# Splitting the position-bias rows of attention 1 into two fp32r parts

## What is computed

```python
def t5_bucket(dist):
    max_exact = N_BUCKETS // 2
    d = jnp.maximum(dist, 0)
    df = jnp.maximum(d, 1).astype(jnp.float32)
    large = max_exact + (jnp.log(df / max_exact) / math.log(MAX_DISTANCE / max_exact)
                         * (N_BUCKETS - max_exact)).astype(jnp.int32)
    return jnp.where(d < max_exact, d, jnp.minimum(large, N_BUCKETS - 1))

    # moba
    s_own = jnp.einsum('bhqd,bhkd->bhqk', qc, ko).astype(jnp.float32) * scale
    s_own = s_own + jnp.take(tab, t5_bucket(t[:, None] - pos_own[None, :]), axis=1)[None]
    s_own = jnp.where(pos_own[None, :] <= t[:, None], s_own, -jnp.inf)
    # dsa: keys picked by the indexer
    bias = jnp.moveaxis(jnp.take(tab, t5_bucket(t[None, :, None] - idx), axis=1), 0, 1)
    s = jnp.where((idx <= t[None, :, None])[:, None], s + bias, -jnp.inf)
```

## Time and profile before

| | us |
|---|---|
| median of 3 runs | 1678.28 |
| lowest, highest | 1676.63, 1682.06 |
| profiled execution (its span) | 1676.6 |
| PE busy in it | 1630.6 (97%) |
| DVE, ACT, POOL busy | 1226.9, 906.6, 430.5 |
| mean granted PE clock | 0.991 of full speed |

### The profile page before, as it was taken

The page is one execution under the profiler, slowest core; times in us unless marked ns, Lnnn a source line. Parts: engine busy times, 40 slices in busy tenths (PEclk is TensorE's granted clock), DMA queues, the critical chain, the costliest instruction groups (busy, mean ns, idle before and its releaser), DMA issues.

```text
span 1676.6 us, 31268 instructions
## 1 busy us (share of the span) xinstructions
PE 1630.6 (97%) x10740; PEld 1437.4 (86%) x10740; DVE 1226.9 (73%) x2406; ACT 906.6 (54%) x1743; POOL 430.5 (26%) x173
## 2 busy tenths in 40 slices
PE   6999899999999999999999999999999999899998
PEld 3976799999999999888888888965799998579997
DVE  4477879689808994877887777767697887776665
ACT  3455554455459996554545545358544445664443
POOL 0970028989985556000000000000200000020000
PEclk9999999999999999999999999999999999999999
DMA  9885885556553334788888885640388766146553
GB/s 346 295 186 193 304 253 178 186 177 186 178 186 114 114 113 146 255 292 284 292 293 286 287 282 166 184 177 1 130 299 288 275 237 152 55 160 188 186 187 103
DMA packets 105526, 344.24 MB, mean 205 GB/s; under 512 B 18484, under 2 KB 22340, under 8 KB 105445
## 3 DMA queue, kind: packets, MB, share of 16 engines
q1 hardware_dynamic: 101092, 339.19, 61.0%
q10 hardware_dynamic: 4352, 4.02, 0.8%
HBM read 341.02 MB, written 1.10 MB: 204 GB/s over the span
## 4 chain that ended last, share of the span: by engine, by line
PE 90%; DVE 3%; ACT 2%; DMA 2%; POOL 1%; issue 1%; ACTq 0%; POOLq 0%; SPq 0%; DVEq 0%
PE banks L673 26%; PE banks L674 25%; PE banks L675 25%; PE banks L1020 3%; PE banks L868 2%; PE banks L835 1%; DMA ring<-in_stream 1%; POOL weights_low L631 1%; PE banks L886 1%; DVE arena L1870 1%; PE banks L845 1%; ACT weights_high L1308 1%; PE banks L706 1%; PE banks L707 1%; ACT arena L1366 1%
## 5 line engine op out<-in xcount | busy, mean ns | idle before, releaser
L1308 ACT ACTIVATE weights_high<-ring 128x1024 fp32r<-128x1024 f32 x470 | 494.8, 1054 | 312.5 <-PE banks L675 299.0
L631 POOL TENSOR_TENSOR weights_low<-ring,weights_high 128x1024 fp32r<-128x1024 f32 x168 | 429.3, 2569 | 669.2 <-ACT weights_high L1308 668.9
L673 PE MATMUL banks<-ht_high,weights_high 128*128 128x256 f32 x1936 | 556.8, 288 | 4.0 <-DVE ht_low L1825 3.9
L674 PE MATMUL banks<-ht_low,weights_high 128*128 128x256 f32 x1936 | 547.9, 283 | 0.0
L675 PE MATMUL banks<-ht_high,weights_low 128*128 128x256 f32 x1936 | 547.8, 283 | 0.0
L1797 DVE TENSOR_TENSOR weights_low<-ring,weights_high 128x1024 fp32r<-128x1024 f32 x302 | 368.2, 1223 | 86.5 <-ACT weights_high L1308 85.6
L673 PEld LDWEIGHTS banks<-ht_high,weights_high 128*128 128x128 f32 x1936 | 371.2, 192 | 7.6 <-issue 4.8
L674 PEld LDWEIGHTS banks<-ht_low,weights_high 128*128 128x128 f32 x1936 | 371.5, 192 | 2.6
L675 PEld LDWEIGHTS banks<-ht_high,weights_low 128*128 128x128 f32 x1936 | 371.1, 192 | 0.0
L1747 DVE SCALAR_TENSOR_TENSOR arena<-arena,cs 128x1024 f32<-128x1024 f32 x80 | 106.9, 1343 | 36.5 <-DMA arena<-in_ada 31.4
L673 PE MATMUL banks<-weights_high,hidden_high 128*128 128x512 f32 x256 | 100.3, 392 | 0.0
(11 more groups left out here) (275 smaller groups left out, 2580.3 us busy)
## 6 DMA issues: line engine op xcount, KB each, us to landing
ring<-in_stream SPq DMA_DIRECT2D x490, 512.0 KB, 3.5
arena<-in_ada SPq DMA_DIRECT2D x88, 512.0 KB, 5.4
ada_ring<-in_ada SPq DMA_DIRECT2D x56, 512.0 KB, 4.2
arena<-gate_store SPq DMA_DIRECT2D x5, 512.0 KB, 6.0
arena<-bias_rows ACTq DMA_DIRECT2D x1, 2048.0 KB, 19.3
X<-in_x SPq DMA_DIRECT2D x1, 1024.0 KB, 5.9
out<-X SPq DMA_DIRECT2D x4, 256.0 KB, 2.1
arena<-arena ACTq DMA_DIRECT2D x8, 127.5 KB, 4.9
```

The source lines that it names most:

```text
L631: pool.tensor_tensor(WL[:, c % SLOTS, :], ring[:, c % SLOTS, :], WH[:, c % HIGHS, :], ALU.subtract)\
L673: pe.matmul(out, wh, xh, start=start, stop=False, **kw)
L674: pe.matmul(out, wh, xl, start=False, stop=False, **kw)
L1308: act.activation(WH[:, c % HIGHS, :], ring[:, c % SLOTS, :], ACT.Copy).then_inc(S["high_ready"], 1)
```

## The change

The rows are split on DVE right after they are made: a high part rounded to fp32r (`ROWS_HIGH`) and the remainder (`ROWS_LOW`). Both go to DRAM, 2 x 24 KB, and come back shifted, the high part as `BIASH` (2 MB) in the place of `BIAS`, the low part in two loads of 1 MB (`BIASL`: heads of moba, heads of dsa). The flipped identity is copied into fp32r (`FLIP`) ahead of the bf16 masks. Each full fp32 bias product becomes two fp32r products, FLIP by BIASH and FLIP by BIASL.

```diff
-        onehot = sb("onehot", [P, ONEHOTS, 2, 4, P])
+        onehot = at("onehot", "onehot", [P, ONEHOTS, 2, 4, P])
-        bias_rows = nc.dram_tensor("bias_rows", (16, ROW_COLS), F32, kind="Internal")
+        bias_rows = nc.dram_tensor("bias_rows", (2, 16, ROW_COLS), F32, kind="Internal")
-        BIAS = A(A_BIAS, 16, T)
+        BIASH = at("bias_high", "arena", [P, 16, T], F32R, 4 * A_BIAS)
+        BIASL = [at("bias_low_moba", "arena", [P, 8, T], F32R, 4 * A_S), at("bias_low_dsa", "onehot", [P, 8, T], F32R)]
+        FLIP = at("flip", "pick", [P, P], F32R)
+        ROWS_HIGH = at("rows_high", "pick", [P, ROW_COLS], F32R, 4 * 128)
+        ROWS_LOW = at("rows_low", "pick", [P, ROW_COLS], F32R, 4 * 512)
...
# PE, scores
-                        m = pe.matmul(o, flip, BIAS[:, first:first + 3:2, T - w:T], start=False, stop=kind == "moba",
-                                      skip_group_check=True)
+                        low = BIASL[first // 8][:, first % 8:first % 8 + 3:2, T - w:T]
+                        pe.matmul(o, FLIP[:], BIASH[:, first:first + 3:2, T - w:T], start=False, stop=False, skip_group_check=True)
+                        m = pe.matmul(o, FLIP[:], low, start=False, stop=kind == "moba", skip_group_check=True)
...
# PE, ahead of attention 1
-            pe.wait_ge(S["bias_loaded"], 16)
-            pe.wait_ge(S["bf16_ready"], 5)
+            pe.wait_ge(S["bias_loaded"], 48)
+            pe.wait_ge(S["bf16_ready"], 6)
...
# ACT
-            act.dma_start(bias_rows.ap(), A(A_R, ROW_COLS)[0:16, :]).then_inc(S["rows_stored"], 16)
+            for i, rows in enumerate([ROWS_HIGH, ROWS_LOW]):
+                act.dma_start(bias_rows.ap()[i], rows[0:16, :].bitcast(F32)).then_inc(S["rows_stored"], 16)
...
-                act.dma_start(BIAS, shifted).then_inc(S["bias_loaded"], 16)
+                act.dma_start(BIASH[:].bitcast(F32), shifted(0, 16)).then_inc(S["bias_loaded"], 16)
+                for i in range(2):
+                    act.dma_start(BIASL[i][:].bitcast(F32), shifted(16 + 8 * i, 8)).then_inc(S["bias_loaded"], 16)
...
# DVE
-                                      A(A_E, 2 * ROW_COLS)[0:16, ROW_COLS:2 * ROW_COLS], ALU.add).then_inc(S["rows_taken"], 1)
+                                           A(A_E, 2 * ROW_COLS)[0:16, ROW_COLS:2 * ROW_COLS], ALU.add))
+                    link(dve.tensor_copy(ROWS_HIGH[0:16, :], A(A_R, ROW_COLS)[0:16, :]))
+                    dve.tensor_tensor(ROWS_LOW[0:16, :], A(A_R, ROW_COLS)[0:16, :], ROWS_HIGH[0:16, :], ALU.subtract).then_inc(S["rows_taken"], 1)
...
+            dve.tensor_copy(FLIP[:], flip).then_inc(S["bf16_ready"], 1)
             dve.tensor_copy(ident_b[:], ident).then_inc(S["bf16_ready"], 1)
```

More of the change, by code:

```diff
@@ L260, in two_blocks @@
         place, size = {}, 0
-        for name, n in [("arena", NKEYS * T), ("ring", SLOTS * D), ("high", HIGHS * D), ("ht", DB * T), ("hth", DB * T), ("pick", 4 * T)]:
+        for name, n in [("arena", NKEYS * T), ("ring", SLOTS * D), ("high", HIGHS * D), ("ht", DB * T), ("hth", DB * T), ("pick", 4 * T), ("onehot", ONEHOTS * 8 * P)]:
             place[name] = size
@@ L1461, in index_keys, with shifted @@
                 act.activation(small[:, 42:44], small[:, 40:42], ACT.Sqrt, scale=1.0 / 64, bias=epsc[:]).then_inc(S["ik_rms"], 1)
-                act.wait_ge(S["rows_stored"], 16)
-                shifted = bass.AP(tensor=bias_rows, offset=0, ap=[[1, P], [ROW_COLS, 16], [1, T]])
-                act.dma_start(BIAS, shifted).then_inc(S["bias_loaded"], 16)
+                act.wait_ge(S["rows_stored"], 32)
+                def shifted(row, n):
+                    return bass.AP(tensor=bias_rows, offset=row * ROW_COLS, ap=[[1, P], [ROW_COLS, n], [1, T]])
+                act.dma_start(BIASH[:].bitcast(F32), shifted(0, 16)).then_inc(S["bias_loaded"], 16)
+                for i in range(2):
+                    act.dma_start(BIASL[i][:].bitcast(F32), shifted(16 + 8 * i, 8)).then_inc(S["bias_loaded"], 16)
             take("qk1", 18, lambda m: QK[:, m, :], scale=lambda m: 0.125 if m < 4 or 8 <= m < 12 else 1.0, between=index_keys)
@@ L1911, in _ @@
                     dve.wait_ge(S["rows_ready"], 1)
-                    dve.tensor_tensor(A(A_R, ROW_COLS)[0:16, :], banks[0:16, 4, 0:ROW_COLS],
-                                      A(A_E, 2 * ROW_COLS)[0:16, ROW_COLS:2 * ROW_COLS], ALU.add).then_inc(S["rows_taken"], 1)
+                    link(dve.tensor_tensor(A(A_R, ROW_COLS)[0:16, :], banks[0:16, 4, 0:ROW_COLS],
+                                           A(A_E, 2 * ROW_COLS)[0:16, ROW_COLS:2 * ROW_COLS], ALU.add))
+                    link(dve.tensor_copy(ROWS_HIGH[0:16, :], A(A_R, ROW_COLS)[0:16, :]))
+                    dve.tensor_tensor(ROWS_LOW[0:16, :], A(A_R, ROW_COLS)[0:16, :], ROWS_HIGH[0:16, :], ALU.subtract).then_inc(S["rows_taken"], 1)
                 c = START_AT["acc", k]
```

## The result

| us | before | after |
|---|---|---|
| median | 1678.74 (4 runs, 1676.63 to 1682.06) | 1687.38 (4 runs, 1686.86 to 1688.29) |
| ratio, 95% interval | | 1.0050 [1.0037, 1.0062] |
| span of the profiled execution | 1676.6 | 1686.0 |
| PE busy in it | 1630.6 | 1631.2 |
| last pass of chunk 4 of product 1 starts, us from the span's start | 56.80 | 67.87 |

The changed kernel is 8.6 us slower, where 3.15 us less was predicted. The profiled execution of after took 1688.3 us for a span of 1686.0, so some 2.3 us lie around a span; the one of before must have been near 1679. The prediction had set it equal to its span, and since its difference was taken off the median, nothing hangs on that.

What follows compares the result with a forecast made beforehand. The kernel was taken as bound by PE, busy 1630.6 of 1676.6 us. Attention 1's savings summed to 3.15 us, with nothing for added work; off the median 1678.28 that gave 1675.1 (68%), range 1669.5 to 1681.

Steps and rivals of the forecast that it cites:

- The step that failed: ACT's queue in product 1: the added loads and store cost 0.40 us of issue each and nothing in time.
- The cover: ACT in product 1: 1.55 us per chunk in which it waits for PE would hide the added issues.
- the unknown price of the products: fp32r passes in attention 1: at best the pace of known passes (taken), at worst a full fp32 product each.
- The slower rival: Product 1, 50 to 90 us: bias loads crowd out weights, PE stops at some 10 chunks, 7 us slower, 1685; 5%.
- The rival by which the passes go at the pace of full fp32: Attention 1: bias products double, 12 us more on PE, perhaps 9 in the time, 1687; 3%.
- The bias products: Attention 1, full clock: 0.73 us instead of 1.13 per 128-key step, 1.18 instead of 1.98 per 256-key step.
- What of it arrives: Attention 1, step by step: 0.25 + 0.8 + 2 x 0.25 + 2 x 0.80 = 3.15 us less.
- the 0.1 to 0.4 given: Start of attention 1: DVE's scaling of step 0 ends 0.25 us earlier, with bounds 0.1 and 0.4.
- ACT or DVE would absorb all but 1 us of the gain: Steps 3 to 7 paced by DVE or ACT, or loads behind attention 1 not moving: about 1 us gained, 1677.3; 14%.
- are kept: Behind attention 1: the following chain and `ring` load move with PE's last products, so the 3.15 us stay.
- The rival by which it slips past POOL: Attention 1: step 0's scalings all start before POOL's first low part, clock stays full, 8.6 us less, 1669.7; 10%.
- The start and the cast: DVE: two small operations at the start cost nothing, at most 0.3 us; the cast before the masks costs nothing.

Runs made afterwards that it cites:

- e6: The changed kernel with the low load of the dsa heads issued behind chunk 8 of product 1, the moba one left in place; 1678.06 us, ratio 0.9992.
- e10: The changed kernel with both low loads replaced by one of 8 KB in 128 pieces, both passes reading the high part; 1679.36 us against 1679.93.
- e11: The changed kernel with its three bias loads reordered, the two low ones first and the high one last; 1679.69 us, ratio 0.9999.
- e3: The changed kernel without low rows or low loads, both fp32r passes reading the high part; 1678.55 us, ratio 0.9993 against the kernel before.
- e7: The changed kernel with the two low loads issued by SP, behind chunk 10's load, instead of by ACT; 1681.65 us, ratio 1.0012.
- e12: The changed kernel with low loads behind chunks 4 and 8 and attention 1's two low parts made by DVE instead of POOL; 1670.59 us, ratio 0.9951.
- e1: The changed kernel with the two low loads issued later, behind chunks 4 and 8 of product 1; 1676.81 us, ratio 0.9987.
- e13: The kernel before, without the change, with attention 1's two low parts made by DVE instead of POOL; 1672.39 us, ratio 0.9953.

## Why the prediction was wrong

**The step that failed** is the one that ended with "Two more loads and one more store on ACT's queue: 0.40 us of issue each, beside 1.55 us in which ACT waits for PE per chunk", and with it the "Nothing" that closes the paragraph. It took 0.40 us for each, and the price was 3.99 and 6.59. PE then waited 8.4 us for ACT. The cover was about right: a hold costs its length less 1.9 us. The holds of 2.70, 3.68 and 3.42 us in e6, e10 and e11 delayed chunk 4 by 0.76, 1.75 and 1.52 us (chunk 4's end less chunk 0's, against 11.67 in before). For after that makes 10.6 - 1.9 = 8.7 us, and 9.9 were measured; the other 1.2 is PE's half clock behind its wait: the 24 passes of chunk 4 start over 4.11 us (63.76 to 67.87) instead of the 2.76 of full clock.

The 0.40 us came from a row, but from one with an empty queue, and no row of before shows an issue behind 2,048 pieces. The prediction bounded the unknown price of the products from both sides, but gave this one no upper bound. A bound was at hand. If ACT can't go on until the load ahead has landed, an issue costs up to the 19.3 us of the earlier trace rows, less the room. That end, even with a small chance, would have put the time that came, 1687, within reach.

**The slower rival** stood at the right place, product 1, with nearly the right size (1685), and its mechanism was wrong. It had chunks of `ring` taking over 11.5 us to land. In after the two that are asked for beside the bias loads, at 52.49 and 55.37 us, land in 7.79 and 8.35 us, against 6.99 and 7.59 for the two at that place in before, and the bias was in by about 71 us, not 89. PE waits for ACT, not for data. The rival by which the passes go at the pace of full fp32 gave 1687 as well, and is refuted by their rows: 0.11 and 0.23 us apart. That 1685 and 1687 lie near the time that came is luck.

**The bias products.** 0.73 and 1.18 us forecast, 0.73 and 1.19 measured.

**What of it arrives.** 3.15 us forecast for attention 1, 2.95 measured (45.21 to 42.26), and 3.12 in e3. Counted from the start of the last pass of product 1, DVE's scaling of step 0 starts 1.20 us earlier than in before, POOL 0.09, and the scaling ends 0.11 earlier, at the low bound of the 0.1 to 0.4 given. The wait at L873 was to be 4.7 us and is 4.76. Nine kernels with the new products and DVE and POOL in their old order show 40.5 to 42.5 us (e7 the least, the others from 41.3), two with the old products 45.21 and 45.38. That ACT or DVE would absorb all but 1 us of the gain in this stage is refuted. That the 3.15 us "are kept" behind the stage isn't shown: the interval of e3 goes from 2.9 us faster to 0.5 slower, and in its profiled execution a stretch of half clock at 1117 to 1124 us takes most of the gain.

**DVE and POOL.** That the scaling of step 0 stays long was right (5.15 us), and so was the reason. The rival by which it slips past POOL needed another order than after's; e7 shows it once, as forecast from the order: 0.88 us with a start 0.8 ahead of POOL's. But its price, 8.6 us with the products' gain, was too high for that case: e7's stage is 4.7 us shorter than before's. PE waits 2.5 and 1.1 us for ACT's exponentials there, its clock falls to 0.50 at 128.3 us all the same, and the scaling of step 1 meets POOL (3.54 us). e12's 1670.59 us lies near the 1669.7 worked out, but there POOL does nothing in the stage, which is another case. The Trainium skill, SBUF — State Buffer, "Who interferes with whom", lets one of the two engines have a shared pair of ports for a whole instruction; the traces agree: scalings of 128 columns take 0.87 and 0.88 us where POOL is idle and 5.15 beside its two low parts, those of 256 columns 1.14 and 5.35.

**The start and the cast.** The two DVE operations were given at most 0.3 us. They take 0.35 and 0.55 us, and the piece behind them starts at 26.07 us, not later than before's. In after chunk 0 ends 1.14 us later than in before (46.27 and 45.13), but this isn't theirs: e1, which has them, ends it at 43.96 and e13, which doesn't, at 46.31. It is likely the landing of the first loads that scatters: ahead of its next piece DVE waits 4.10 us for one in after and 3.30 in before. The cast of `FLIP` takes 0.22 us; two mask casts behind it take 2.42 and 2.40 us beside POOL, as forecast, and nobody waits for them.

**The range** was too narrow by 6 us at the top, and the 7% for slower too low. Nearly all of both came from the cost put at nothing.

## What to carry to other kernels

In these kernels the price of a DMA issue depends on what its engine has issued just before: up to about 1,000 pieces not yet landed it costs 0.4 to 0.7 us, behind 2,000 it costs 2.4 to 7.6 (in between the runs differ), and everything that this engine computes stands behind it. So ahead of a load that is added to the queue of a computing engine, count the pieces (contiguous runs, not bytes) of the loads ahead of it, put a few chunks of work between them, and put the load with the most pieces last. Where a price is read off a row, look whether the resource was empty in that row.

## What the runs showed that I had not expected

- An 8 KB load took 3.68 us to issue behind one of 2,048 pieces, as long as a load of 1 MB (3.99). With 1 KB pieces 10.6 us of holds, with 512-byte pieces 9.6.
- The hold belongs to the issuing engine's own queue: SP issued in 0.65 us at 52.01 us, while ACT's load of 2,048 pieces of 50.38 us was on its way. In after SP issued at 52.49 us in 0.33 us, while ACT was held.
- Issuing 2,048 pieces onto an empty queue takes 0.40 us, as 1,024 do.
- While ACT was held, DMA traffic ran at 370 GB/s and a DMA share of 1.04 to 1.07: the stall doesn't show as an idle or a slow DMA.
